# Attention with rotary embedding: the halves exchanged by small DMAs instead of a permutation matmul, q rotated at another place of a head, another order of the prologue

## The reference

```python
def rot(xa, pos):
    ang = pos[:, None] * inv[None, :]
    x1, x2 = xa[..., :nf], xa[..., nf:]          # nf = 16
    return jnp.concatenate([x1 * cos - x2 * sin, x2 * cos + x1 * sin], axis=-1)
...
s = jnp.einsum('bqhmd,bkhmd->bhmqk', qi, k) * scale     # two score maps a head, m = 0, 1
p = jax.nn.softmax(s, axis=-1)
a = p[:, :, 0] - lam * p[:, :, 1]
o = jnp.einsum('bhqk,bkhd->bqhd', a, v)
```

## Time and profile before

| | before |
|---|---|
| median of 3 runs | 1927.57 us (1925.98 to 1928.19) |
| profiled execution | 1926.9 us, span 1925.1 us |
| PE busy | 1784.5 us, 93% |
| VectorE, ScalarE, GpSimd busy | 1021.5, 698.4, 652.9 us |
| chain that ended last | PE 86%, VectorE 6%, ScalarE 3% |
| PE psT L739 (the swap matmul) in that chain | 1% |

### The profile page before, as it was taken

The page is one execution under the profiler, slowest core; times in us unless marked ns, Lnnn a source line. Parts: engine busy times, 40 slices in busy tenths (PEclk is TensorE's granted clock), DMA queues, the critical chain, the costliest instruction groups (busy, mean ns, idle before and its releaser), DMA issues.

```text
span 1925.1 us, 30275 instructions
## 1 busy us (share of the span) xinstructions
PE 1784.5 (93%) x11636; PEld 1666.2 (87%) x11636; DVE 1021.5 (53%) x1547; ACT 698.4 (36%) x1074; POOL 652.9 (34%) x286
## 2 busy tenths in 40 slices
PE   6999999769899999999996999998889999999995
PEld 3688888658899999999996889887779999999995
DVE  2476766544755612655427535534548771277724
ACT  3245554433522211222226435545253331133323
POOL 3212122225643332333444222112455333333441
PEclk8999999789899999999998999999989999999998
DMA  9511111002254222543220111110112222122221
GB/s 385 215 52 50 41 50 50 28 12 76 89 195 168 97 75 77 184 167 134 89 65 28 50 50 55 50 50 28 55 45 77 71 83 76 58 73 76 80 73 55
DMA packets 50072, 165.08 MB, mean 86 GB/s; under 512 B 5696, under 2 KB 11328, under 8 KB 49984
## 3 DMA queue, kind: packets, MB, share of 16 engines
q1 hardware_dynamic: 43648, 159.68, 24.1%
q10 hardware_dynamic: 6336, 4.20, 0.7%
HBM read 159.12 MB, written 4.74 MB: 85 GB/s over the span
## 4 chain that ended last, share of the span: by engine, by line
PE 86%; DVE 6%; ACT 3%; issue 2%; DVEq 2%; DMA 1%; POOL 0%; ACTq 0%; SPq 0%; POOLq 0%
PE pj L565 71%; PE mO L975 2%; PE psS L714 2%; PE psO L756 2%; PE pfrow L604 1%; PE psT L730 1%; DMA awr<-in_w_ada 1%; PE prow L588 1%; PE psT L739 1%; DVE pr L1808 1%; PE mS L931 1%; PE mT L938 1%; PE pfmod L611 1%; PE pmod L595 1%; PE psT L764 1%
## 5 line engine op out<-in xcount | busy, mean ns | idle before, releaser
L453 POOL TENSOR_TENSOR wlo<-wraw,whi 128x1024 fp32r<-128x1024 f32 (+1 forms) x130 | 343.6, 2643 | 868.3 <-ACT whi L1107 868.3
L565 PE MATMUL pj<-Hh,whi 128*128 128x322 f32 x2400 | 579.3, 323 | 52.4 <-issue 18.8
L565 PE MATMUL pj<-Hl,whi 128*128 128x322 f32 x2400 | 560.3, 315 | 0.0
L565 PE MATMUL pj<-Hh,wlo 128*128 128x322 f32 x2400 | 556.0, 313 | 0.0
L565 PEld LDWEIGHTS pj<-Hh,whi 128*128 128x128 f32 x2400 | 407.1, 192 | 82.8 <-issue 55.7
L565 PEld LDWEIGHTS pj<-Hl,whi 128*128 128x128 f32 x2400 | 412.6, 192 | 0.0
L565 PEld LDWEIGHTS pj<-Hh,wlo 128*128 128x128 f32 x2400 | 412.3, 192 | 0.0
L1107 ACT CAST whi<-wraw 128x1024 fp32r<-128x1024 f32 (+1 forms) x182 | 201.7, 1108 | 342.4 <-PE pj L565 298.1
L1669 DVE SCALAR_TENSOR_TENSOR X<-pj,mods,X 128x129 f32<-128x129 f32 (+1 forms) x144 | 54.6, 435 | 283.9 <-PE pj L565 283.8
L1722 DVE SCALAR_TENSOR_TENSOR fcv<-fus,vec,fcv 128x644 f32<-128x644 f32 x88 | 176.2, 2002 | 15.0 <-issue 15.0
L565 PE MATMUL pj<-Gh,whi 128*128 128x322 f32 x704 | 162.4, 312 | 0.0
(11 more groups left out here) (310 smaller groups left out, 2122.8 us busy)
## 6 DMA issues: line engine op xcount, KB each, us to landing
wraw<-in_w_up SPq DMA_DIRECT2D x88, 512.0 KB, 3.5
fwr<-in_w_ada SPq DMA_DIRECT2D x56, 512.0 KB, 5.5
wraw<-in_w_dn SPq DMA_DIRECT2D x32, 704.0 KB, 4.1
awr<-in_w_ada SPq DMA_DIRECT2D x40, 512.0 KB, 10.1
wraw<-in_w_qkv SPq DMA_DIRECT2D x24, 512.0 KB, 3.5
wraw<-in_w_mlin SPq DMA_DIRECT2D x24, 512.0 KB, 3.5
wraw<-in_w_wo SPq DMA_DIRECT2D x8, 512.0 KB, 3.4
wraw<-in_w_mlout SPq DMA_DIRECT2D x8, 512.0 KB, 3.4
```

Of the source, the lines that this page charges most:

```text
L453: nc.gpsimd.tensor_tensor(wlo[k][:, 0:width], wraw[k][:, 0:width], whi[k][:, 0:width].bitcast(F32), ALU.subtract).then_inc(w_lo, 1)
L565: last = mm(out[:, c, 0:HALF], w, x[:, j, c * HALF:(c + 1) * HALF], start=(j == 0 and n == 0), stop=(j == n_k - 1 and n == 2))
```

## The change

PE no longer swaps. SP does, with eight DMAs for one swap: each copies 16 partitions by 512 columns (32 KB) from `h32t` to the neighbouring group's place in `sx`. `rotate` then reads both its operands from SBUF. In a head `rotate("q", h+1)` and `q_lo(h+1)` stand later on VectorE, and `q_hi(h+1)` stands later on ScalarE, directly before a cast of weights. In the prologue `ada_block(5)` and `ada_turn(4)` come before `qkv(2, ...)`, units 2 and 3 are loaded earlier, and some row copies move. SP's run of weight loads is written out, with the swaps between.

```diff
--- before.py
+++ after.py
@@ -82,16 +82,11 @@
 
 def _turn_uses():
 
-    order = [("q", 0), ("k", 0)]
+    order = []
     for h in range(DA_HEADS):
         if h:
             order.append(("t", 5 * h - 1))
-        if h < DA_HEADS - 1:
-            order.append(("q", h + 1))
-        order += [("v", h), ("t", 5 * h), ("t", 5 * h + 1), ("t", 5 * h + 2)]
-        if h < DA_HEADS - 1:
-            order.append(("k", h + 1))
-        order.append(("t", 5 * h + 3))
+        order += [("v", h), ("t", 5 * h), ("t", 5 * h + 1), ("t", 5 * h + 2), ("t", 5 * h + 3)]
         if h:
             order.append(("r", h - 1))
     order += [("t", 5 * DA_HEADS - 1), ("r", DA_HEADS - 1)]
...
@@ -383,24 +377,38 @@
                 for k in range(2):
                     load(w[bass.ds(2 * i + k + at, 1)].rearrange("a p n -> p (a n)"), base // 2 + i, k, width)
 
+            def swap(n, w):
+
+                sp.wait_ge(pj_copied, 3 * n + w + 1)
+                if 2 * n + w > 0:
+                    sp.wait_ge(roped, 2 * n + w)
+                half = DK // 4
+                for b in range(P // half):
+                    c = b ^ 1
+                    sp.dma_start(sx[half * b:half * (b + 1), 0:LAT], h32t[half * c:half * (c + 1), w, L0:L0 + LAT]).then_inc(swapped, 16)
+
             load_ada(range(11))
             load_qkv(0)
             load_qkv(1)
             load_ada(range(11, 16))
             for j in range(KT):
                 sp.dma_start(X[:, j, :], a["xT"][:, j]).then_inc(xin[j], 16)
+            load_qkv(2)
+            load_qkv(3)
             load_ada(range(16, 27))
-            sp.dma_start(perm[:, :], a["mats"][:, 1]).then_inc(perm_in, 16)
             sp.dma_start(rope[:, :, :], a["rope"]).then_inc(rope_in, 16)
-            load_qkv(2)
-            load_ada(range(27, 31))
-            load_qkv(3)
-            load_ada(range(31, 39))
+            swap(0, 0)
+            load_ada(range(27, 35))
+            swap(0, 1)
+            load_ada(range(35, 39))
             load_qkv(4)
             load_ada(range(39, 4 * NB))
             load_qkv(5)
-            load_run(a["w_qkv"], 6, 3 * DA_HEADS - 6, D, at=6)
-            load_run(a["w_wo"], U_WO, KT, D)
+            for v in range(6, U_WO + 2):
+                load(a["w_qkv"][v] if v < U_WO else a["w_wo"][v - U_WO], v // 2, v % 2, D)
+                if v % 3 < 2:
+                    swap(v // 3 - 1, v % 3)
+            load_run(a["w_wo"], U_WO + 2, KT - 2, D, at=2)
 
             def load_ffn(layer, base):
                 for half in range(2):
...
@@ -731,13 +739,6 @@
                                                pr[idx % 2][:, 0, c * P:(c + 1) * P], ident[:, :])
                 last.then_inc(t_full, 1)
 
-            def swap(which, n):
-
-                pe.wait_ge(pj_copied, 3 * n + (1 if which == "q" else 2))
-                t_wait(USE[which, n])
-                src = h32[0] if which == "q" else h32[1]
-                mm(psT[:, 0, :], perm[:, :], src[:, L0:L0 + LAT], start=True, stop=True).then_inc(t_full, 1)
-
             def values_ctx(h):
                 par = h % 2
                 pe.wait_ge(t_free, USE["t", 5 * h] + 1)
...
@@ -789,7 +790,6 @@
                     turn(h - 1, 4)
                 if nxt:
                     qkv(k, [0, 1])
-                    swap("q", h + 1)
                 if prev:
                     values_lat(h - 1)
                 scores(h, 1)
...
@@ -815,9 +815,7 @@
                     qkv(v, [4])
                 turn(h, 2)
                 if nxt:
-                    qkv(v, [5, 6])
-                    swap("k", h + 1)
-                    qkv(v, [7])
+                    qkv(v, [5, 6, 7])
                 if last:
                     wo([4, 5])
                 scores(h, 4)
...
@@ -833,15 +831,12 @@
 
             first_pair(0, KT, h_ready, 0, reads=((), ()))
             ada_block(4)
-            pe.wait_ge(perm_in, 16)
-            swap("q", 0)
-            swap("k", 0)
-            qkv(2, [0, 1, 2, 3])
             ada_block(5)
             ada_turn(4)
-            qkv(2, [4, 5, 6, 7])
+            qkv(2, [0, 1, 2, 3])
             ada_block(6)
             ada_turn(5)
+            qkv(2, [4, 5, 6, 7])
             qkv(3, [0, 1])
             ada_block(7)
             ada_turn(6)
...
@@ -1305,7 +1300,6 @@
                 exps(h, 0)
                 if nxt:
                     unit_split(v)
-                    q_hi(h + 1)
                 else:
                     act.wait_ge(tile_done, 3 * DA_HEADS)
                     output_hi(O32, onorm, (0, 1))
...
@@ -1325,6 +1319,7 @@
                 exps(h, 2)
                 o_out(h, (C0, C0 + CTX), 0)
                 if nxt:
+                    q_hi(h + 1)
                     unit_split(q2)
                 else:
                     output_hi(O32, onorm, (4, 5))
...
@@ -1348,11 +1343,11 @@
             copy_q(0)
             copy_kv(0, 0, h32[1])
             unit_split(2)
+            unit_split(3)
             q_hi(0)
-            unit_split(3)
             cache_hi(0)
+            copy_kv(0, 1, v32)
             k_hi(0)
-            copy_kv(0, 1, v32)
             unit_split(4)
             for h in range(DA_HEADS):
                 head(h)
...
@@ -1820,10 +1815,10 @@
 
             def rotate(which, n):
 
-                src = h32[0] if which == "q" else h32[1]
-                dve.wait_ge(t_full, USE[which, n] + 1)
-                tt(sx[:, 0:LAT], psT[:, 0, :], rope[:, 1, :], ALU.mult).then_inc(t_free, 1)
-                x = src[:, L0:L0 + LAT]
+                w = "qk".index(which)
+                dve.wait_ge(swapped, 16 * 8 * (2 * n + w + 1))
+                tt(sx[:, 0:LAT], sx[:, 0:LAT], rope[:, 1, :], ALU.mult)
+                x = h32[w][:, L0:L0 + LAT]
                 tt(x, x, rope[:, 0, :], ALU.mult)
                 dve.drain()
                 tt(x, x, sx[:, 0:LAT], ALU.add).then_inc(roped, 1)
...
@@ -1862,16 +1857,16 @@
                 if prev:
                     turned(h - 1, 4)
                 combine(h, 0)
-                if nxt:
-                    rotate("q", h + 1)
                 nmax(h, 1)
                 values_lo(h)
                 turned(h, 0)
+                combine(h, 1)
+                if nxt:
+                    rotate("q", h + 1)
+                nmax(h, 2)
+                turned(h, 1)
                 if nxt:
                     q_lo(h + 1)
-                combine(h, 1)
-                nmax(h, 2)
-                turned(h, 1)
                 combine(h, 2)
                 nmax(h, 3)
                 turned(h, 2)
...
@@ -1886,13 +1881,15 @@
                     normalise(h - 1)
 
             copy_rows(4)
+            copy_rows(5)
             dve.wait_ge(rope_in, 16)
             rotate("q", 0)
             q_lo(0)
+            copy_rows(6)
             rotate("k", 0)
-            copy_rows(5)
+            copy_rows(7)
             k_lo(0)
-            for n in range(6, NB):
+            for n in range(8, NB):
                 copy_rows(n)
             dve.wait_ge(row_turned, NB)
             add_bias(pmod, 2 * KT, 4 * NB)
```

More of the change, by code:

```diff
@@ L225, in hybrid_step @@
             ckv = sb("ckv", [P, 2, P], F32, s)
-            perm = sb("perm", [P, P], F32, s)
             sm = sb("sm", [P, 16], F32, s)
@@ L292, in hybrid_step @@
             mO = ps("mO", [P, 2, 512], s)
-        vec_in, const_in, perm_in, rope_in, ckv_in = (
-            sem(n) for n in ("vec_in", "const_in", "perm_in", "rope_in", "ckv_in"))
+        vec_in, const_in, rope_in, ckv_in, swapped = (
+            sem(n) for n in ("vec_in", "const_in", "rope_in", "ckv_in", "swapped"))
         w_landed = [sem(f"w_landed{k}") for k in range(2)]
```

## The result

The changed kernel takes 1929.05 us (median of 20 runs, 1926.99 to 1932.23), the kernel before 1925.76 on the same chip (20 runs, 1923.90 to 1928.19). The ratio is 1.0018, 95% interval 1.0011 to 1.0025. So the change makes the kernel a little slower, by an interval that leaves out zero. The forecast was 1928.0, with a chance of 0.36 for "within 0.2%"; the full return of 1911 was not reached. The profiled execution has a span of 1926.6 us, that of before 1925.1.

What follows compares the result with a forecast made beforehand. PE bounds the kernel, until VectorE's and ScalarE's chain becomes slower. Against the profiled 1926.9: prologue -2.0, five heads +3.0, one -0.5, the seventh 0, giving 1927.4; median 1928. Range 1911 to 1935, likeliest 1924 to 1932.

Steps and rivals of the forecast that it cites:

- within 0.2%: Whole kernel: no change that a measurement can tell, 0.2% being about 3.9 us; chance 0.36.
- the full return of 1911: Rival: VectorE gets in before GpSimd in `combine(h, 2)`, PE waits nowhere, 16.7 us comes back: 1911; chance 0.2.
- The swap on PE: Heads: two swaps leave PE, 2.1 us a head, a ceiling of 14.7 us for seven heads.
- The DMAs: Swap on SP's queue: 0.35 us an issue, 1.6 to landing, last landing 4.4 after the start, waits covered.
- a sign of being wrong: The prediction is wrong if VectorE waits for `swapped`, or if GpSimd starts after `combine(h, 2)`'s last operation in a head.
- I cost SP at nothing: SP's queue: the loads behind the swaps wait for GpSimd anyway, so the swaps' issues cost nothing.
- The collision: `combine(h, 2)`, every head: GpSimd's subtraction starts 0.6 us before VectorE's large last operation, which waits; PE idles 1.9 us.
- the case that the scaling waits: `combine(h, 2)`: the scaling ahead of the last operation waits too, ending at 229.8 not 229.5, 0.3 us more a head.
- The head: One head, first scores to next: 0.5 us shorter without a clock fall, 0.6 longer than before with one.
- The clock: PE's granted clock falls after the 1.9 us idle in five of six full heads, each 1.1 us longer than without.
- The seventh head: Last of the seven heads: PE has no next q to make and hangs on VectorE; gain 0.
- The prologue: Before the first scores: block 5 fits in front (2.81 us), less the copy's wait (0.70 and 0.1): -2.0 us.

Runs made afterwards that it cites:

- e7: The kernel before, swaps still by matmul on PE, with e1's later order of q's rotation, `q_hi` and `q_lo`: 1926.42 us, ratio 1.0004.
- e1: The changed kernel with `q_lo` moved from ahead of `combine(h, 2)` to behind the low part of a head's last transposes: 1909.53 us, ratio 0.9921.
- e2: The changed kernel with eight unread matmuls added on PE ahead of `turn(h, 2)`, filling its wait: 1924.47 us, ratio 0.9998.
- e4: The changed kernel with GpSimd subtracting only 8 of 1024 columns for later heads' q units and two output units: 1910.4 us, ratio 0.9926.
- e8: e1's kernel with the prologue's last modulation load issued ahead of the load of unit 4: 1908.11 us, ratio 0.9917.
- e3: The changed kernel with q's rotation, `q_hi` and `q_lo` back at their old places, swaps still by DMA: 1921.83 us, ratio 0.9985.
- e5: The changed kernel with each swap in 16 DMAs of 16 KB in place of eight of 32 KB: 1941.82 us, ratio 1.0082.
- e9: e8's kernel with block 7 and its transposes ahead of unit 3's first two pieces on PE: 1911.32 us, ratio 0.9928.

## Why the prediction was right, point by point

The mechanism that the prediction called decisive came as forecast: GpSimd gets in ahead of VectorE in every head, and the swaps' gain is lost. That the sum came within about 1 us is luck in part, since two terms that it had wrong or left out nearly cancelled (the last point below).

**The swap on PE.** The forecast was 2.1 us a head, 14.7 at most. e7 against e1 gives 2.3 a head, and 274.27 - 258.41 = 15.9 for the seven heads. The term was right, a little small.

**The DMAs.** The forecast was 0.35 us for an issue and 1.6 to landing; 0.59 and 2.0 were measured, and a swap takes 6.3 us and not 4.4. The terms were too small, and the swaps were covered all the same. VectorE did wait for `swapped`, which the prediction named as a sign of being wrong, but only in the prologue and beside work of PE. "I cost SP at nothing" holds in the heads. In the prologue the last modulation load was late and its block took 2.75 us in place of 1.90, which the prediction missed. Another cost was not foreseen: ScalarE's eight issues of `ckv` from `cache_v` take 0.45 to 1.21 us (0.45 to 1.30 in e1), where they take 0.45 to 0.46 before. The one of 1.21 stands at 215.89, between two swaps and not beside one (the swap ahead of it had landed by 210.84), so why it is long stays open.

**The collision.** The forecast was that GpSimd is 0.6 us ahead of the large last operation in every head. It is there in every head, 0.69 us ahead of where that operation would have started, and already 0.06 to 0.07 us ahead of the scaling. By the prediction's own clock the scaling would have stood at 226.08 (0.62 us ahead of the last operation's 226.7) against GpSimd's 226.1, a tie, and the prediction left open whether the scaling waits as well. `combine(h, 2)` ended 26.39 us into the head; the forecast was 229.5 - 203.47 = 26.03, with 26.33 for the case that the scaling waits. PE's wait was forecast at 1.9 us and is 1.97. e1, e2 and e4 show that it is this pair: taken apart on either engine, the time is 1910 us; kept, it is 1924 to 1929.

**The head.** The forecast was 0.5 us shorter without a fall of the clock and 0.6 longer with one. Against before's 39.8 to 40.0 the heads are 0.1 to 0.3 shorter or 0.6 to 0.9 longer. The difference is about the 0.3 to 0.4 us by which the combination ends later.

**The clock.** The forecast was a fall in five of the six full heads, each costing 1.1 us. Three of six have one, and it costs 0.8 to 1.1 us; the same wait brings one or doesn't. Head 0, which the prediction counts among the six, had none behind its collision, but one at 87.8 us, as it had one at 89.4 in e1, so it isn't the change's collision that brought that one. It is 0.85 longer than before all the same. Heads 0 to 5 together take 2.83 us more, against a forecast of 2.5. The sum is right partly by luck, since too many falls, too much gain without a fall and head 0's other fall cancelled.

**The seventh head.** The forecast was 0, since it "hangs on VectorE". It is 1.8 us shorter in both pairs of profiles. This step failed: e7 against e1 gives it the full 2.2 us of its swaps, so PE sets its length too.

**The prologue.** The forecast was -2.0. The first scores stand at 85.04 and 86.19 against 87.86 and 87.97: -2.8 and -1.8. Unit 2 starts at 56.84 and 57.58, and the first scores follow 28.20 and 28.61 us later. Before, it started at 58.91 and 59.01 (PE's timeline; the chain of the earlier trace rows has 59.07) and the scores followed 28.95 later. So this part gave back only 0.3 to 0.8. Of the 2.81 us of block 5, 0.88 went to the copy's wait, 0.85 to the last block's late load (e8 takes it away) and 0.2 to block 6, which took 2.11 and not 1.90. The rest of the gain is unit 2's earlier start, which the prediction had held fixed. Unit 2 starts 4.8 us behind the end of the first pair of units in every profile, and that end stands at 51.97 in place of 54.07; the mean clock of the first 56 us was 0.88 there and 0.85 before. How much of this belongs to the change is not shown: e7 has the old prologue, and its pair ends 0.7 earlier than before's at 53.34, and with the new prologue's order unit 2 starts at 56.06 in e2 and at 58.77 in e3. The forecast was right in the sum, not in the place.

**What the sum left out.** Prologue and heads of the first pair are -2.8 + 1.0 = -1.8 us, yet the span grew by 1.5: +3.3 came behind the last head's start (1566.8 us against 1563.5), nearly all of it in the first 70 us, where the clock falls again and again. The second pair gives -1.8, +0.9 and +2.7, about +1.9 in all. That term had no place in the forecast. It was cancelled in part by the seventh head's -1.8 and, in the first pair, by the prologue's 0.8 beyond the forecast. Why it comes is open: e1, e4 and e8 don't have it, e5 and e9 do. The medians lie 3.3 us apart and the spans only 1.5 to 1.9, because both profiles of before are of executions above that kernel's median (1926.9 and 1927.3 us against 1925.76) and the first one of the changed kernel is of one below its own (1928.39 against 1929.05).

## What to carry to other kernels

When work leaves the bounding engine, follow the chain that the freed time runs into, event by event, and look for two operations of VectorE and GpSimd that are released by the same event: here GpSimd came 0.7 us ahead of VectorE's last operation in every head, which decided between 1929 and 1910 us, and moving one operation of 0.83 us undid it. Such a margin has to be counted to the last operation of the chain and not to its first, since GpSimd also gets into the gap between two of them. An order that a wait made harmless before may be harmful after. And a swap by DMA is not free for its queue: eight issues cost 4.9 us and the last one lands 6.3 us behind the first issue, in one case 7.9. So give it a place with that much cover, and see what loads stand behind it.

## What was not expected of the hardware

- A scaling with a single SBUF tensor input and 640 columns waits for GpSimd's subtraction as the two-input operations do: 2.67 to 2.69 us in place of 0.55, seven times of seven. The rows of before showed only the two-input case. The Trainium skill (SBUF — State Buffer, section SBUF: two separate sides) names VectorE's 2-port modes beside the two-input case; the runs show the wait and not the mode.
- GpSimd starts in the gap of 0.07 us between two operations of VectorE (120.01 between 119.98 and 120.05), and the second of them takes 3.03 us in place of 0.89.
- The same idle time of 1.95 to 1.97 us is followed by a fall of TensorE's clock in three of six heads, and not in the same ones in the next profile. Each of these falls lasts 3.4 us, and a head with one is 0.8 to 1.1 us longer.
- An issue of a DMA from SBUF to SBUF over 16 partitions takes SP 0.59 us in the median with 32 KB, and with 16 KB the same 0.59.
